# Sparse prompt attention taken head by head, with wide value products

## The chip, the cores and the metric

The kernel runs on one core of a Trainium2 chip. The metric is the device time of one execution in microseconds (us), as the median of several runs; lower is better. The core has a matmul engine (TensorE, PE in the rows, with its weight loads as PEld), a vector engine (VectorE, DVE), an activation engine (ScalarE, ACT), GpSimd (POOL) and a sync engine (SyncE, SP), which in this kernel issues almost all loads. Each engine works through its own list of instructions in order; they meet only through semaphores.

## The reference

One inference step of a four-layer decoder: gated linear attention (layer 0), sparse softmax attention (layer 1), a pooling mixer (layer 2) and gated linear attention again (layer 3). It is computed for a prompt of 512 tokens and for 8 x 4 sample tokens that look back on 1024 cached positions in pages. The change lies in layer 1, in the attention of the prompt:

```
def sparse_attend(q, k_sel, v_sel, valid):
    s = jnp.einsum('bqhd,bqkhd->bqhk', q, k_sel) * (DSA_HEAD_DIM ** -0.5)
    s = jnp.where(valid[:, :, None, :], s, -jnp.inf)
    p = jax.nn.softmax(s, axis=-1)
    return jnp.einsum('bqhk,bqkhd->bqhd', p.astype(v_sel.dtype), v_sel)

def dsa_out(o, g, w_out):
    B, L = o.shape[:2]
    return (o.reshape(B, L, DSA_WIDTH) * jax.nn.silu(g)) @ w_out
```

There are 8 heads of 128 numbers; each query keeps the 128 keys that an indexer scores highest among those not after it. The kernel does not gather keys for the prompt: it scores all keys that are not after the query's tile and adds a bias of -1e30 to those that were not chosen.

## The kernel before

**Units.** The 512 queries are four tiles of 128 (t = 0 to 3). A unit is one query tile of one head: 32 units. A unit of tile t has t + 1 key tiles. The list `UNITS` (lines 80 and 81) sets the order for every engine: four heads at a time of one query tile, the eight groups being (1, heads 0 to 3), (3, 0 to 3), (0, 0 to 3), (2, 0 to 3), then (0, 4 to 7), (1, 4 to 7), (2, 4 to 7), (3, 4 to 7).

**Steps of a unit.** `scores(n)` (PE, L1405) multiplies queries and keys, a product of 128(t + 1) columns; `shift(n)` (DVE, L2628 and L2633) adds the bias, writes `att_p` and takes the row maximum; the exponential (ACT, L2006) follows; `normalise(n)` (DVE, L2639 and L2641) divides by the row sum; `probs(n)` (PE, L1413) turns the t + 1 blocks of 128 x 128; `pt_out(n)` (ACT, L1979, in the profile the helper's line L1532) copies the turned blocks from PSUM to `att_pt`; `values_of(n)` (PE, L1424) multiplies them with the values, t + 1 products of 128 columns. Each fp32 product shows as two matmul passes in the trace, each turn as one.

**Groups of four units.** Four units fill one PSUM bank of 512 columns. Then comes the branch: DVE multiplies with the gate (L2649), ACT writes the high part `h_hi` (`branch_hi`, L1985, shown as L1532), DVE the low part `h_lo` (L2239). DVE waits for ACT between its two instructions.

**Order in time.** All engines run one loop over n. In step n, PE does scores(n), then a value page if there is one, then probs(n-2), then values_of(n-3). DVE does shift(n), normalise(n-1), and in every fourth step a branch. ACT does the exponential of n, pt_out(n-2), and in every fourth step branch_hi.

**Value pages.** Between the units PE works for the sample tokens. In the steps n = 0, 1, 3, 5 ... 29 it multiplies one page of cached values for each of four sequences (`value_page`, L1441): 16 steps with a page, each taking four transfers of 512 KB that SP issues as buffers come free. After the 8th and 16th page come the products with the new keys (L1448); in step 15 the sample probabilities of the second group are turned (L1380, L1382), in steps 17 and 33 the sample output (`turn_out`, L1458).

**After it.** `out_proj` multiplies the gated output with the output weights: three products for each of 8 k-blocks of 128 (one k-block is one head), L780 to L782. Its first half of the tokens (columns 0 to 271) waits for the branch of group (2, heads 4 to 7), its second for the last branch. In step 31 ACT also splits the first output weights (`w_hi`, L1532, 128x1024), from which POOL computes `w_lo` (L744).

Of the kernel before, what the change touches and what calls it, by code (L numbers as in the profile page):

```python
# [14 lines left out]
F32 = mybir.dt.float32  # L15
# [3 lines left out]
ALU = mybir.AluOpType  # L19
# [59 lines left out]

QUADS = [(1, 0), (3, 0), (0, 0), (2, 0), (0, 1), (1, 1), (2, 1), (3, 1)]  # L80
UNITS = [(t, 4 * half + h) for t, half in QUADS for h in range(4)]

# [11 lines left out]
def program(nc, plan, x_prompt, x_sample, state_gla, cache_k, cache_v, cache_idx_k, state_pool, page_table,  # L94
# [5 lines left out]
    with ExitStack() as ctx:  # L100
# [150 lines left out]
        v_end = d.o  # L251
        bias_p = [None] + [d(f"dsa_bias{t}", [P, P * (t + 1)]) for t in range(1, NP_T)]
        bias_s = d("dsa_bias_s", [NS, KEYS], BF16)
        ast = d("dsa_ast", [P, 5, 4])
# [7 lines left out]
        kst_at = d.o  # L262
        k_st = d("dsa_k_st", [P, TILES, BLK])
        tmp_d = d("dsa_tmp", [P, BLK])
        tmp_d2 = d("dsa_tmp2", [P, 8 * NS])
# [15 lines left out]
        a = Region(kst_at, kst_end)  # L281
        p_at = a("att_p", [P, 3, BLK])
        pt_at = a("att_pt", [P, 2, BLK])
        a = Region(pt_s_at, kst_end)
# [469 lines left out]
        def _(pe):  # L754
# [171 lines left out]
            def out_proj(L, between=None):  # L926
                last = L == len(KINDS) - 1

                def ready(k, part):
                    if KINDS[L] == 2:  # L930
                        pe.wait_ge(*on("h_lo", L, "y", k))
                    elif KINDS[L] == 0 and part == 0 and k % 4 == 0:
                        pe.wait_ge(*on("h_lo", (L, "out"), 2, k // 4))
                    elif k == 0 and KINDS[L] == 0:
                        pe.wait_ge(*on("h_lo", (L, "out"), SMP, 1))
                    elif k == 0:
                        pe.wait_ge(*on("h_lo", (L, "out"), *(QUADS[-2] if part == 0 else (SMP, 1))))

# [278 lines left out]
            def dsa(L):  # L1217
# [190 lines left out]
                def probs(n):  # L1408
                    t, h = units[n]
                    b = claim(2 + n % 2, ("PT", L, n), ("PT_read", L, n))  # L1410
                    pe.wait_ge(*on("p_norm", L, n))
                    for s in range(t + 1):
                        mm = pe.transpose(psum[:, b, s * P:(s + 1) * P], p_at[:, n % 3, s * P:(s + 1) * P], ident[:])  # L1413
                    mm.then_inc(*sig("PT", L, n))

                def values_of(n):
                    t, h = units[n]
                    m = n // 4
                    b = 4 + m % 2
                    if n % 4 == 0:  # L1420
                        claim(b, ("O", L, m), ("oT_read", L, t, h // 4))
# [40 lines left out]
                for n in range(N + 3):  # L1462
                    if n == 2 * NPAGE - 1:
                        turn_probs(1, (0, 1, 2))
                    if n in (2 * NPAGE + 1, 4 * NPAGE + 1):
                        turn_out(n // (4 * NPAGE))
                    if n < N:
                        scores(n)
                    if (n == 0 or n % 2) and n < 4 * NPAGE - 1:
                        value_page((n + 1) // (2 * NPAGE), (n + 1) // 2 % NPAGE)  # L1470
                    if 2 <= n <= N + 1:
                        probs(n - 2)
                    if n >= 3:
                        values_of(n - 3)
                out_proj(L)
# [54 lines left out]
        def _(act):  # L1530
# [277 lines left out]
            def dsa(L):  # L1808
# [165 lines left out]
                def pt_out(n):  # L1974
                    t, h = units[n]
                    act.wait_ge(*on("PT", L, n))
                    if n >= 2:
                        act.wait_ge(*on("O", L, n - 2))
                    copy(pt_at[:, n % 2, 0:(t + 1) * P], psum[:, bank_of("PT", L, n), 0:(t + 1) * P])\  # L1979
                        .then_inc(*sig("PT_read", L, n))  # L1980

                def branch_hi(m):
                    t, h = units[4 * m]
                    act.wait_ge(*on("oT_read", L, t, h // 4))
                    copy(H[L % 2][0][:, h:h + 4, cols(t)], tmp_d[:].rearrange("p (k t) -> p k t", k=4))\  # L1985
                        .then_inc(*sig("h_hi", (L, "out"), t, h // 4))

# [3 lines left out]
                for n in range(len(units) + 4):  # L1991
# [10 lines left out]
                    if n < len(units):  # L2002
                        t, h = units[n]
                        act.wait_ge(*on("s_shift", L, n))
                        x = p_at[:, n % 3, 0:(t + 1) * P]
                        act.activation(x, x, ACT.Exp, bias=ast[:, n % 3, 1:2], scale=score_scale[:, 0, t:t + 1],  # L2006
# [85 lines left out]
        def _(dve):  # L2092
# [124 lines left out]
            def resid(L):  # L2217
# [15 lines left out]
                input_lo(L + 1, *order[-1])  # L2233

            def out_lo(L, t, half, tmp):
                k = slice(4 * half, 4 * half + 4)
                dve.wait_ge(*on("h_hi", (L, "out"), t, half))
                hi, lo = H[L % 2]
                dve.tensor_tensor(lo[:, k, cols(t)], tmp.rearrange("p (k t) -> p k t", k=4),  # L2239
                                  hi[:, k, cols(t)].bitcast(F32), ALU.subtract)\  # L2240
                    .then_inc(*sig("h_lo", (L, "out"), t, half))


# [241 lines left out]
            def dsa(L):  # L2485
# [135 lines left out]
                def shift(n):  # L2621
# [4 lines left out]
                    if n >= 3:  # L2626
                        dve.wait_ge(*on("PT", L, n - 3))
                    dve.tensor_tensor_reduce(out=p_at[:, n % 3, 0:w], in0=psum[:, bank_of("S", L, n), 0:w],  # L2628
                                             in1=(bias_p[t][:] if t else future_p[:]), scale=1.0, scalar=TAKEN,
# [6 lines left out]
                def normalise(n):  # L2636
                    t, h = units[n]
                    dve.wait_ge(*on("p_exp", L, n))
                    link(dve.reciprocal(ast[:, n % 3, 3:4], ast[:, n % 3, 2:3]))  # L2639
                    x = p_at[:, n % 3, 0:(t + 1) * P]  # L2640
                    dve.tensor_scalar(x, x, ast[:, n % 3, 3:4], None, ALU.mult).then_inc(*sig("p_norm", L, n))  # L2641

                def branch(m):
                    t, h = units[4 * m]
                    dve.wait_ge(*on("O", L, 4 * m + 3))
                    if m:
                        pt, ph = units[4 * m - 4]
                        dve.wait_ge(*on("h_lo", (L, "out"), pt, ph // 4))
                    dve.tensor_tensor(tmp_d[:].rearrange("p (k t) -> p k t", k=4),  # L2649
                                      psum[:, 4 + m % 2, :].rearrange("p (k t) -> p k t", k=4),  # L2650
                                      gate_d[:, h:h + 4, cols(t)], ALU.mult).then_inc(*sig("oT_read", L, t, h // 4))
                    out_lo(L, t, h // 4, tmp_d[:])

# [136 lines left out]
```

## Time and profile before

| | us |
|---|---|
| median of 3 runs | 1143.22 |
| lowest and highest | 1142.87 and 1147.44 |
| profiled execution | 1143.32 |
| its span in the trace | 1141.6 |
| PE busy in it | 1107.5 (97%) |
| DVE busy | 669.8 (59%) |
| ACT busy | 490.9 (43%) |
| POOL busy | 381.8 (33%) |

The busy time of an engine is the time in which any of its instructions runs. Matmuls overlap, so the busy share of PE says little about how full it is; the distance from one start to the next is what a matmul costs. The stretch that the change touches lies from 576.4 us (first scores) to about 670 us of the span. In it the transfers of the cached values run as well.

### The profile page before, as it was taken

What the parts mean: (1) busy time and instruction counts of PE and PEld (TensorE: products, weight loads), DVE (VectorE), ACT (ScalarE), POOL (GpSimd) and SP (SyncE); (2) the same over time, 40 slices, a digit from 0 to 9 for tenths busy, and PEclk for the clock granted to TensorE, in tenths of its full rate; (3) what the DMA queues carried; (4) which work ended last, traced back from release to release, by engine and by line L of the source; (5) the groups of instructions that cost most, each with busy time, mean ns of one, the idle gap of its engine ahead of it and who ended that gap; (6) DMA issues with size and microseconds to landing.
All of it is one profiled execution on the core that took longest, in us unless ns stands there. A gap on an engine that the chain in (4) does not pass through costs nothing. (4 is left out here: it accounts for less than half of the span.)

```text
span 1141.6 us, 25758 instructions
## 1 busy us (share of the span) xinstructions
PE 1107.5 (97%) x10659; PEld 967.4 (85%) x10659; DVE 669.8 (59%) x1215; ACT 490.9 (43%) x960; POOL 381.8 (33%) x321
## 2 busy tenths in 40 slices
PE   8999999899999999999998999999999999999997
PEld 6889888899758988878954599999999889988796
DVE  6362355854999789677444646596455272255742
ACT  6542376643434222222364554332454352467643
POOL 5545122243313423114300044354335245312330
PEclk9999999999999999999999999999999999999998
DMA  5235234232315776894779942233220335233302
GB/s 177 99 112 166 92 111 147 97 100 87 118 46 185 240 266 212 272 319 147 259 292 409 373 125 79 71 111 95 101 94 3 111 112 157 84 130 112 105 26 79
DMA packets 126747, 168.97 MB, mean 148 GB/s; under 512 B 19336, under 2 KB 92336, under 8 KB 126623
## 3 DMA queue, kind: packets, MB, share of 16 engines
q1 hardware_dynamic: 114569, 152.75, 40.1%
q10 hardware_dynamic: 12062, 14.59, 3.6%
q8 instruction: 84, 1.38, 0.5%
q14 instruction: 32, 0.26, 0.1%
HBM read 150.86 MB, written 16.81 MB: 147 GB/s over the span
## 5 line engine op out<-in xcount | busy, mean ns | idle before, releaser
L744 POOL TENSOR_TENSOR w_lo<-raw,w_hi 128x512 fp32r<-128x512 f32 x265 | 358.0, 1383 | 681.0 <-ACT w_hi L1532 680.8
L780 PE MATMUL psum<-h_hi,w_hi 128*128 128x272 f32 x1584 | 462.0, 292 | 6.3 <-DVE h_lo L2449 4.7
L782 PE MATMUL psum<-h_hi,w_lo 128*128 128x272 f32 x1584 | 458.0, 289 | 0.0
L781 PE MATMUL psum<-h_lo,w_hi 128*128 128x272 f32 x1584 | 455.7, 288 | 0.0
L780 PEld LDWEIGHTS psum<-h_hi,w_hi 128*128 128x128 f32 x1584 | 297.3, 188 | 19.8 <-issue 14.7
L781 PEld LDWEIGHTS psum<-h_lo,w_hi 128*128 128x128 f32 x1584 | 297.7, 188 | 0.1
L782 PEld LDWEIGHTS psum<-h_hi,w_lo 128*128 128x128 f32 x1584 | 296.9, 187 | 0.0
L1532 ACT ACTIVATE w_hi<-raw 128x1024 fp32r<-128x1024 f32 (+1 forms) x135 | 133.3, 1033 | 111.5 <-PE psum L782 77.1
L780 PE MATMUL psum<-w_hi,h_hi 128*128 128x512 f32 (+2 forms) x352 | 124.6, 354 | 0.0
L782 PE MATMUL psum<-w_hi,h_lo 128*128 128x512 f32 (+2 forms) x352 | 121.0, 344 | 0.7 <-issue 0.7
L781 PE MATMUL psum<-w_lo,h_hi 128*128 128x512 f32 (+2 forms) x352 | 121.1, 344 | 0.4 <-issue 0.4
L2560 DVE STREAM_TRANSPOSE smp_keys<-smp_keys 128x2048 f32<-128x2048 f32 x32 | 73.1, 2301 | 34.1 <-DMA smp_keys<-in_cache_k_dram 33.8
L2227 DVE TENSOR_TENSOR XT<-psum,XT 128x272 f32<-128x272 f32 x64 | 27.9, 440 | 87.9 <-PE psum L782 87.9
L780 PEld LDWEIGHTS psum<-w_hi,h_hi 128*128 128x128 f32 (+1 forms) x352 | 64.0, 182 | 15.5 <-issue 5.8
L782 PEld LDWEIGHTS psum<-w_hi,h_lo 128*128 128x128 f32 (+1 forms) x352 | 64.1, 182 | 9.4 <-issue 0.5
L781 PEld LDWEIGHTS psum<-w_lo,h_hi 128*128 128x128 f32 (+1 forms) x352 | 64.1, 182 | 7.8
L1532 ACT ACTIVATE h_hi<-XT,gains 128x272 fp32r<-128x272 f32 x48 | 25.1, 523 | 75.1 <-DVE XT L2227 75.1
L1345 PE MATMUL psum<-smp_keys,raw 32*32 32x256 f32 x2048 | 46.2, 385 | 4.6 <-DVE smp_keys L2560 2.4
L1345 PEld LDWEIGHTS psum<-smp_keys,raw 32*32 32x32 f32 x2048 | 29.4, 103 | 16.4 <-issue 7.0
L2158 DVE TENSOR_TENSOR sq_sum<-sq_sum,sq_new 128x272 f32<-128x272 f32 x54 | 42.3, 783 | 1.5 <-ACT sq_new L1605 1.5
L1532 ACT ACTIVATE gla_s_now<-gla_s_now,gla_fac 128x256 f32<-128x256 f32 x64 | 27.2, 496 | 34.7 <-DVE gla_s_now L2332 25.9
L2549 DVE MAX8 dsa_top<-dsa_score_s 32x8 f32<-32x1056 f32 x32 | 39.6, 1238 | 0.8
(333 smaller groups left out, 1381.5 us busy)
## 6 DMA issues: line engine op xcount, KB each, us to landing
smp_keys<-in_cache_k_dram SPq DMA_DIRECT2D x128, 256.0 KB, 4.5
raw<-in_gla_w_in_dram SPq DMA_DIRECT2D x23, 1024.0 KB, 5.4
raw<-in_dsa_w_in_dram SPq DMA_DIRECT2D x17, 1024.0 KB, 5.5
spare<-in_cache_v_dram SPq DMA_DIRECT2D x34, 512.0 KB, 8.1
raw<-in_cache_v_dram SPq DMA_DIRECT2D x30, 512.0 KB, 8.4
gla_s_in<-in_state_gla_dram SPq DMA_DIRECT2D x16, 512.0 KB, 7.7
raw<-in_gla_w_out_dram SPq DMA_DIRECT2D x8, 1024.0 KB, 6.6
out_dram<-gla_s_in ACTq DMA_DIRECT2D x16, 512.0 KB, 4.7
```

The source lines that it names most:

```text
L744: pool.tensor_tensor(pair_view(w_lo, key)[:, k], raw_view(key)[:, k], pair_view(w_hi, key)[:, k].bitcast(F32), ALU.subtract)\
L780: pe.matmul(out, lh, rh, start=start, stop=False)
L781: pe.matmul(out, lh, rl, start=False, stop=False)
L782: return pe.matmul(out, ll, rh, start=False, stop=stop)
L1345: mm = pe.matmul(psum[band(c), 2 + i, 0:2 * P], q_bands[band(i), j, c, bl, :], keys[band(i), :, c, j, :], start=first and j == 0, stop=Fal ...
L1532: return act.activation(out, in_, ACT.Copy, scale=scale)
L2158: dve.tensor_tensor(sq_sum[:, c], sq_sum[:, c], sq_new[:, blocks(L).index((m, part)) % 2, :], ALU.add)\
L2227: dve.tensor_tensor(XT[:, m, c], psum[:, bank_of("proj", name, part), 0:HC], XT[:, m, c], ALU.add)\
L2549: link(dve.max(out=top8[0:m, :], in_=scores))
L2560: dve.transpose(held(s), held(s)).then_inc(*sig("kt_s", L, u))
```

## The change

The units are taken head by head, each head with tiles 1, 2, 3, 0. The four units of a head are copied into one buffer `att_pt` of 5 x 384 columns, so laid out that the turned probabilities of all query tiles that see key tile x stand side by side: 512 columns for x = 0, then 384, 256 and 128. `values_of` is called once a head, in the steps n = 6, 10 ... 34, with four products of these widths in place of ten of 128 columns. The first copy of a head waits until the value products of the head before are done. The branch works on one head and all 512 tokens, and `out_proj` waits for the branch of each head at its k-block, in the first half of the tokens. The third `att_p` buffer now lies where `bias_s` was. The numbers of passes and columns of scores and turns are the same as before.

```diff
-QUADS = [(1, 0), (3, 0), (0, 0), (2, 0), (0, 1), (1, 1), (2, 1), (3, 1)]
-UNITS = [(t, 4 * half + h) for t, half in QUADS for h in range(4)]
+UNITS = [(t, h) for h in range(DH) for t in (1, 2, 3, 0)]
...
-        pt_at = a("att_pt", [P, 2, BLK])
+        p_at = [a("att_p0", [P, BLK]), a("att_p1", [P, BLK]), at("att_p2", [P, BLK], F32, bias_s_at)]
+
+        pt_at = a("att_pt", [P, 5, BLK - P])
+        pt_row = pt_at[:].rearrange("p a b -> p (a b)")
...
+                    elif KINDS[L] == 1 and part == 0:
+                        pe.wait_ge(*on("h_lo", (L, "out"), "head", k))
                     elif k == 0:
-                        pe.wait_ge(*on("h_lo", (L, "out"), *(QUADS[-2] if part == 0 else (SMP, 1))))
+                        pe.wait_ge(*on("h_lo", (L, "out"), SMP, 1))
...
-                    pe.wait_ge(*on("PT_read", L, n))
-                    for s in range(t + 1):
-                        mm = pe.matmul(psum[:, b, (h % 4) * P:(h % 4 + 1) * P], v_d[:, s, h * HD:(h + 1) * HD],
-                                       pt_at[:, n % 2, s * P:(s + 1) * P], start=s == 0, stop=s == t)
-                    mm.then_inc(*sig("O", L, n))
+                def values_of(h):
+                    b = claim(4 + h % 2, ("O", L, h), ("oT_read", L, h))
+                    pe.wait_ge(*on("PT_read", L, NP_T * h + NP_T - 1))
+                    for x in range(NP_T):
+                        mm = pe.matmul(psum[:, b, x * P:], v_d[:, x, h * HD:(h + 1) * HD],
+                                       pt_row[:, x * BLK:x * BLK + BLK - x * P], start=x == 0, stop=x == NP_T - 1,
+                                       skip_group_check=True)
+                    mm.then_inc(*sig("O", L, h))
...
-                    if n >= 3:
-                        values_of(n - 3)
+                    if n >= 6 and n % NP_T == 2:
+                        values_of((n - 6) // NP_T)
...
-                    if n >= 2:
-                        act.wait_ge(*on("O", L, n - 2))
+                    if n and n % NP_T == 0:
+                        act.wait_ge(*on("O", L, n // NP_T - 1))
+                    c = t * P % (BLK - P)
+                    copy(pt_at[:, t // 3:t // 3 + t + 1, c:c + P],
...
+                def branch(h):
+                    dve.wait_ge(*on("O", L, h))
+                    if h:
+                        dve.wait_ge(*on("h_lo", (L, "out"), "head", h - 1))
+                    dve.tensor_tensor(tmp_d[:], psum[:, 4 + h % 2, :], gate_d[:, h, 0:SEQ], ALU.mult)\
+                        .then_inc(*sig("oT_read", L, h))
```

**PE between two value pages.** The names: `dsa_k,dsa_q` are scores, `ident,att_p` turns, `att_pt,dsa_v` values, `spare,smp_pt` or `raw,smp_pt` a value page. Before, steps 25 to 27:

```order
L1405 MATMUL psum<-dsa_k,dsa_q 128x384
L1441 MATMUL psum<-spare,smp_pt 32x512 x8
L1413 MATMUL psum<-ident,att_p 128x128 x2
L1424 MATMUL psum<-att_pt,dsa_v 128x128 x2
L1405 MATMUL psum<-dsa_k,dsa_q 128x384
L1413 MATMUL psum<-ident,att_p 128x128 x3
L1424 MATMUL psum<-att_pt,dsa_v 128x128 x2
L1405 MATMUL psum<-dsa_k,dsa_q 128x384
L1441 MATMUL psum<-raw,smp_pt 32x512 x8
```

The same steps now:

```order
L1410 MATMUL psum<-dsa_k,dsa_q 128x384
L1443 MATMUL psum<-spare,smp_pt 32x512 x8
L1418 MATMUL psum<-ident,att_p_162 128x128
L1410 MATMUL psum<-dsa_k,dsa_q 128x512
L1418 MATMUL psum<-ident,att_p_160 128x128 x2
L1425 MATMUL psum<-att_pt,dsa_v 128x512
L1425 MATMUL psum<-att_pt,dsa_v 128x384
L1425 MATMUL psum<-att_pt,dsa_v 128x256
L1425 MATMUL psum<-att_pt,dsa_v 128x128
L1410 MATMUL psum<-dsa_k,dsa_q 128x128
L1443 MATMUL psum<-raw,smp_pt 32x512 x8
```

Every second gap between two pages now holds the value products of a whole head, the others none.

**PE behind the last value page.** Before, from the products with the new keys (`dsa_v,smp_ptn`) to the last value product, which `out_proj` follows; `ident,smp_p` is `turn_out`:

```order
L1448 MATMUL psum<-dsa_v,smp_ptn 32x512 x8
L1413 MATMUL psum<-ident,att_p 128x128 x3
L1424 MATMUL psum<-att_pt,dsa_v 128x128 x3
L1405 MATMUL psum<-dsa_k,dsa_q 128x512
L1413 MATMUL psum<-ident,att_p 128x128 x4
L1424 MATMUL psum<-att_pt,dsa_v 128x128 x3
L1405 MATMUL psum<-dsa_k,dsa_q 128x512
L1413 MATMUL psum<-ident,att_p 128x128 x4
L1424 MATMUL psum<-att_pt,dsa_v 128x128 x4
...
L1458 MATMUL psum<-ident,smp_p_151 128x128 x8
L1413 MATMUL psum<-ident,att_p 128x128 x4
L1424 MATMUL psum<-att_pt,dsa_v 128x128 x8
```

And now:

```order
L1450 MATMUL psum<-dsa_v,smp_ptn 32x512 x8
L1418 MATMUL psum<-ident,att_p_160 128x128
L1410 MATMUL psum<-dsa_k,dsa_q 128x512
L1418 MATMUL psum<-ident,att_p_161 128x128 x2
L1425 MATMUL psum<-att_pt,dsa_v 128x512
...
L1410 MATMUL psum<-dsa_k,dsa_q 128x128
L1418 MATMUL psum<-ident,att_p_162 128x128 x3
L1418 MATMUL psum<-ident,att_p_160 128x128 x4
L1460 MATMUL psum<-ident,smp_p_151 128x128 x8
L1418 MATMUL psum<-ident,att_p_161 128x128
L1425 MATMUL psum<-att_pt,dsa_v 128x512
...
```

Behind the last page stand now 5 score tiles, 11 turns and the values of two heads (20 tiles), before 8, 19 (with one row of four left out above) and 22.

**ACT at the end.** `h_hi<-dsa_tmp` is branch_hi, `w_hi<-raw` the split of the output weights. Before:

```order
L2006 ACTIVATE att_p,dsa_ast<-att_p,dsa_ast,score_scale 128x512
L1532 ACTIVATE att_pt<-psum 128x512
L1532 ACTIVATE h_hi<-dsa_tmp 128x4x128
L1532 ACTIVATE w_hi<-raw 128x1024 x2
L1532 ACTIVATE att_pt<-psum 128x512 x2
```

Now:

```order
L2008 ACTIVATE att_p_161,dsa_ast<-att_p_161,dsa_ast,score_scale 128x128
L1534 ACTIVATE att_pt<-psum 128x3x128
L1534 ACTIVATE h_hi<-dsa_tmp 128x512
L1534 ACTIVATE w_hi<-raw 128x1024 x2
L1534 ACTIVATE att_pt<-psum 128x4x128
L1534 ACTIVATE att_pt<-psum 128x128
```

The places are the same; the last unit is now a small one, and all value products of the last head come behind its copy.

## Rows read from the trace of the kernel before

**Rows 1.** The page's head: span.

```profile
span 1141.6 us, 25758 instructions
```

**Rows 2.** Busy time by stretch; us, engines, granted clock, DMA share, GB/s.

```profile
core 0: us, PE busy (x) PEld busy (x) DVE busy (x) ACT busy (x) POOL busy (x), PEclk, DMA share, GB/s
...
590.00:610.00 20.00, 17.93 (x137) 10.77 (x130) 10.31 (x40) 8.77 (x22) 0.00 (x0) 1.00 1.03 409
...
620.00:640.00 20.00, 19.26 (x154) 10.95 (x147) 12.18 (x57) 9.75 (x30) 0.00 (x0) 1.00 1.02 402
```

**Rows 3.** Waits from 588 to 615 us: total, times, longest.

```profile
PE psum L1441 <- DMA raw<-in_cache_v_dram: 1.9, 2, 1.1
...
PE psum L1441 <- DMA spare<-in_cache_v_dram: 1.0, 2, 0.7
```

**Rows 4.** PE in order of time: start, us, instruction, [idle before <-releaser].

```profile
610.01 1.92 PE L1441 MATMUL psum<-raw,smp_pt 128*32 128x512 f32 x16 [1.09 <-DMA raw<-in_cache_v_dram]
...
625.85 1.92 PE L1441 MATMUL psum<-spare,smp_pt 128*32 128x512 f32 x16
...
649.53 1.02 PE L1405 MATMUL psum<-dsa_k,dsa_q 128*128 128x512 f32 x2
650.40 0.49 PE L1413 MATMUL psum<-ident,att_p 128*128 128x128 f32 x3
650.72 0.83 PE L1424 MATMUL psum<-att_pt,dsa_v 128*128 128x128 f32 x6
651.39 1.02 PE L1405 MATMUL psum<-dsa_k,dsa_q 128*128 128x512 f32 x2
652.35 0.62 PE L1441 MATMUL psum<-raw,smp_pt 128*32 128x512 f32 x2
...
656.05 0.55 PE L1413 MATMUL psum<-ident,att_p 128*128 128x128 f32 x3
...
657.11 1.02 PE L1405 MATMUL psum<-dsa_k,dsa_q 128*128 128x512 f32 x2
...
665.54 2.05 PE L1424 MATMUL psum<-att_pt,dsa_v 128*128 128x128 f32 x16 [0.34 <-ACT att_pt L1532]
667.34 0.37 PE L780 MATMUL psum<-h_hi,w_hi 128*128 128x272 f32 x1
```

**Rows 5.** Line L1413 (turns) in two stretches: PE, PEld busy (x), clock, DMA.

```profile
625.85:652.35 26.50, 4.91 (x24) 2.92 (x24) 1.00 0.98 379
652.35:667.34 14.99, 3.01 (x19) 2.12 (x19) 1.00 0.50 159
```

**Rows 6.** Line L1424 (value passes) in the same two stretches.

```profile
625.85:652.35 26.50, 7.32 (x48) 6.42 (x48) 1.00 0.98 379
652.35:667.34 14.99, 5.76 (x44) 5.24 (x44) 1.00 0.50 159
```

**Rows 7.** Waits from 576 to 676 us, DVE for ACT in the branch.

```profile
DVE h_lo L2239 <- ACT h_hi L1532: 10.2, 8, 1.7
```

**Rows 8.** DVE in order of time, at the end.

```profile
658.17 0.69 DVE L2628 CUSTOM_DVE_ANT_0 att_p<-psum,dsa_bias 128x512 f32<-128x512 f32 x1 [4.17 <-PE psum L1405]
...
661.08 0.15 DVE L2639 RECIPROCAL dsa_ast<-dsa_ast 128x1 f32<-128x1 f32 x1
...
661.67 0.68 DVE L2649 TENSOR_TENSOR dsa_tmp<-psum,dsa_gate 128x512 f32<-128x512 f32 x1
...
669.02 0.81 DVE L2239 TENSOR_TENSOR h_lo<-dsa_tmp,h_hi 128x512 fp32r<-128x512 f32 x1 [0.70 <-ACT h_hi L1532]
```

**Rows 9.** ACT in order of time, at the end.

```profile
662.49 0.62 ACT L1532 ACTIVATE h_hi<-dsa_tmp 128x512 fp32r<-128x512 f32 x1
663.01 1.99 ACT L1532 ACTIVATE w_hi<-raw 128x1024 fp32r<-128x1024 f32 x2
664.90 1.07 ACT L1532 ACTIVATE att_pt<-psum 128x512 f32<-128x512 f32 x2
```

**Rows 10.** Weight loads of the value passes, 576 to 676 us: busy, mean ns.

```profile
L1424 PEld LDWEIGHTS psum<-att_pt,dsa_v 128*128 128x128 f32 x160 | 20.5, 193 | 1.5 <-ACT att_pt L1532 0.9 <-issue 0.5
```

More of the change, by code:

```diff
@@ L252, in program @@
         bias_p = [None] + [d(f"dsa_bias{t}", [P, P * (t + 1)]) for t in range(1, NP_T)]
+        bias_s_at = d.o
         bias_s = d("dsa_bias_s", [NS, KEYS], BF16)
@@ L263, in program @@
         k_st = d("dsa_k_st", [P, TILES, BLK])
+        d.o += size([P, P], F32)
         tmp_d = d("dsa_tmp", [P, BLK])
@@ L281, in program @@
         a = Region(kst_at, kst_end)
-        p_at = a("att_p", [P, 3, BLK])
-        pt_at = a("att_pt", [P, 2, BLK])
+        p_at = [a("att_p0", [P, BLK]), a("att_p1", [P, BLK]), at("att_p2", [P, BLK], F32, bias_s_at)]
+        pt_at = a("att_pt", [P, 5, BLK - P])
+        pt_row = pt_at[:].rearrange("p a b -> p (a b)")
         a = Region(pt_s_at, kst_end)
@@ L1412, in probs @@
                     for s in range(t + 1):
-                        mm = pe.transpose(psum[:, b, s * P:(s + 1) * P], p_at[:, n % 3, s * P:(s + 1) * P], ident[:])
+                        mm = pe.transpose(psum[:, b, s * P:(s + 1) * P], p_at[n % 3][:, s * P:(s + 1) * P], ident[:])
                     mm.then_inc(*sig("PT", L, n))
[L1416 to L1421, printed above, removed]
-                    pe.wait_ge(*on("PT_read", L, n))
-                    for s in range(t + 1):
-                        mm = pe.matmul(psum[:, b, (h % 4) * P:(h % 4 + 1) * P], v_d[:, s, h * HD:(h + 1) * HD],
-                                       pt_at[:, n % 2, s * P:(s + 1) * P], start=s == 0, stop=s == t)
-                    mm.then_inc(*sig("O", L, n))
+                def values_of(h):
[6 more added lines that the diff above has]
+                    mm.then_inc(*sig("O", L, h))
                 def value_page(grp, pg):
@@ L1976, in pt_out, with branch_hi @@
                     act.wait_ge(*on("PT", L, n))
-                    if n >= 2:
-                        act.wait_ge(*on("O", L, n - 2))
-                    copy(pt_at[:, n % 2, 0:(t + 1) * P], psum[:, bank_of("PT", L, n), 0:(t + 1) * P])\
-                        .then_inc(*sig("PT_read", L, n))
[L1982 to L1986, printed above, removed]
+                    if n and n % NP_T == 0:
+                        act.wait_ge(*on("O", L, n // NP_T - 1))
+                    c = t * P % (BLK - P)
+                    copy(pt_at[:, t // 3:t // 3 + t + 1, c:c + P],
+                         psum[:, bank_of("PT", L, n), 0:(t + 1) * P].rearrange("p (x q) -> p x q", q=P))\
+                        .then_inc(*sig("PT_read", L, n))
+                def branch_hi(h):
+                    act.wait_ge(*on("oT_read", L, h))
+                    copy(H[L % 2][0][:, h, 0:SEQ], tmp_d[:]).then_inc(*sig("h_hi", (L, "out"), "head", h))
                 for q in (KT - 2, KT - 1):
@@ L2004, in dsa @@
                         act.wait_ge(*on("s_shift", L, n))
-                        x = p_at[:, n % 3, 0:(t + 1) * P]
+                        x = p_at[n % 3][:, 0:(t + 1) * P]
                         act.activation(x, x, ACT.Exp, bias=ast[:, n % 3, 1:2], scale=score_scale[:, 0, t:t + 1],
@@ L2233, in resid @@
                 input_lo(L + 1, *order[-1])
[L2235 to L2241, printed above, removed]
             def gla(L):
@@ L2627, in shift @@
                         dve.wait_ge(*on("PT", L, n - 3))
-                    dve.tensor_tensor_reduce(out=p_at[:, n % 3, 0:w], in0=psum[:, bank_of("S", L, n), 0:w],
+                    dve.tensor_tensor_reduce(out=p_at[n % 3][:, 0:w], in0=psum[:, bank_of("S", L, n), 0:w],
                                              in1=(bias_p[t][:] if t else future_p[:]), scale=1.0, scalar=TAKEN,
@@ L2639, in normalise @@
                     link(dve.reciprocal(ast[:, n % 3, 3:4], ast[:, n % 3, 2:3]))
-                    x = p_at[:, n % 3, 0:(t + 1) * P]
+                    x = p_at[n % 3][:, 0:(t + 1) * P]
                     dve.tensor_scalar(x, x, ast[:, n % 3, 3:4], None, ALU.mult).then_inc(*sig("p_norm", L, n))
[L2643 to L2652, printed above, removed]
+                def branch(h):
[4 more added lines that the diff above has]
+                        .then_inc(*sig("oT_read", L, h))
+                    hi, lo = H[L % 2]
+                    dve.wait_ge(*on("h_hi", (L, "out"), "head", h))
+                    dve.tensor_tensor(lo[:, h, 0:SEQ], tmp_d[:], hi[:, h, 0:SEQ].bitcast(F32), ALU.subtract)\
+                        .then_inc(*sig("h_lo", (L, "out"), "head", h))
                 for n in range(len(units) + 4):
```

## The prediction

> **What bounds the kernel now.** First the page's head and the times: the profiled execution took 1143.32 us, of which the span is 1141.6 [rows 1]; the 1.7 us around it stay. The median of the runs shown, 1143.22, is 0.1 us below this execution, so the sum is made against 1143.3.
>
> Second, the busy time by stretch [rows 2]. Between 590 and 640 us the transfers are busy all the time (share 1.02 to 1.03, 402 to 409 GB/s). One value page is 4 x 512 KB = 2.1 MB, at 408 GB/s 5.1 us. Third: who waits for whom between 588 and 615 us [rows 3]. PE waits for value pages four times, 2.9 us in all, and the last wait ends at 610.01, at the 8th page [rows 4]. Up to there the transfers set the pace. After it no value page begins with a wait for a transfer: PE has become the slower one, and it stays so.
>
> Fourth, PE in order of time [rows 4], read by distances of starts, since busy times overlap. Scores of 512 columns are two passes in 650.40 - 649.53 = 0.87 us, or 0.435 a pass and 0.109 for 128 columns. Three turns take 650.72 - 650.40 = 0.32, 0.107 each. Six value passes of 128 columns take 651.39 - 650.72 = 0.67, 0.112 each. A value page takes 1.85 (half of the 3.70 from 652.35 to 656.05, in which a page and the equally long products with the new keys stand). DVE and ACT have idle time there, but their latency shows at the end: at 665.54 PE waits for the last copy, then the last value passes run and out_proj starts at 667.34. From 667.34 on PE is busy without a gap for long, so a later out_proj is a later end of the kernel, one for one.
>
> **The change part by part.** The kernel is cut at 610.01, 625.85 (10th page), 652.35 (16th page) and 667.34.
>
> *Fewer, wider value passes.* 160 passes of 128 columns (80 tiles by two) become 64. One head costs 2 x (512+384+256+128)/512 x 0.435 = 2.18 us; ten tiles narrow cost 20 x 0.112 = 2.24. That is 0.06 a head, 0.4 us for all eight. The weight loads that go (96 of 193 ns, [rows 10]) ran beside passes that start every 112 ns, so they save nothing more.
>
> *Up to 610.01.* A head now costs PE between two equal points two pages 3.7, ten score tiles 2.18, ten turns 1.07, the values 2.18 and about 0.3 of changes between kinds of work: 9.4 us, against 10.3 us for the transfers of two pages. So the 8th page still waits for its transfer, with some 0.8 us to spare. 0 us; bounds -0.3 (the wait was 1.1 and cannot turn into a gain, the next transfer has its own time) and +1.0 (if the first head, whose exponentials start late, stalls).
>
> *610.01 to 625.85.* Scores of steps 14 to 17: before tiles 3, 3, 1, 1 = 8, now 4, 1, 2, 3 = 10: +0.44. Turns 10 and 10. Values: before units 10 to 13 = 8 tiles, 16 x 0.112 = 1.79, now head 2 = 2.18: +0.39. In step 17 turn_out must wait until DVE has read the scores of step 16, and DVE does this behind a branch, in which it stands 10.2 / 8 = 1.3 us for ACT [rows 7]. Before, value passes of 0.67 us stood in PE's list ahead of turn_out; now none do. I take +0.6 (bounds 0 and 1.2). Sum +1.4.
>
> *625.85 to 652.35.* This is the cleanest comparison. The page steps are 17 and 29. Scores are 30 tiles before and after. Turns: 24 before [rows 5], now those of units 15 to 26 in the new order, 30: +0.64. Values: 48 passes before [rows 6], 5.38 us, now heads 3, 4, 5 = 6.54: +1.16. So PE reaches the last page with more of the units done, 1.8 us later. A loop beside it: turn, copy, branch_hi, the low part, the next two maxima, the exponential, the copy, the values. By the durations of the kinds of rows shown in [rows 8, 9] it comes to about 9.5 us a head, as long as PE's own 9.4. I add 0.2. Sum +2.0 (bounds 0 and 4).
>
> *652.35 to 667.34: 14.99 us before.* What was done earlier is now missing here: 5 score tiles in place of 8, 11 turns in place of 19, 20 value tiles in place of 22. By PE's work alone, 3.70 + 5 x 2 x 0.109 + 11 x 0.107 + 2 x 2.18 + turn_out's eight turns 0.95 = 11.3 us, 3.7 us less. But the chain cannot be that short. From the page's start: 3.70; turn 0.17, scores of unit 30 0.87, two turns 0.22, head 6 2.18, scores of unit 31 0.22: 7.4. DVE, 0.2 later, needs about 0.5 for the small maximum and its scaling, 0.59 for normalising unit 30 (661.08 to 661.67, [rows 8]) and 0.68 for the branch of head 6: 9.4. ACT: branch_hi 0.52 (662.49 to 663.01), the split of the weights 1.89 (663.01 to 664.90), the copies of units 30 and 31 some 0.5 and 0.25 [rows 9]: 12.7. Then all four products of head 7, 2.18: 14.9. So out_proj begins 14.9 after the page, -0.1 us. All the work taken out of this stretch becomes waiting. Bounds -1.5 (if ACT comes by its branch_hi earlier) and +2 (if the copy of unit 31 meets a late DVE).
>
> *out_proj's new waits.* The k-block of head 7 is the last of eight; it is asked for 21 products later, 2.6 us at the measured rate of three products per 0.375. Before, from 667.34 to the end of the last low part (669.02 + 0.81 = 669.83, [rows 8]) 2.5 us pass. It just fits: 0, bounds 0 and +0.5. Gate, branch and low part have the same number of elements, and the copy to `att_pt` the same columns: 0.
>
> Sum: 0 + 1.4 + 2.0 - 0.1 = +3.3, on the span 1144.9, as a time 1146.6. Against the median shown this is +3.4, or 0.3%.
>
> A rule of the Trainium skill speaks against this sum. Its page "TensorE: Matmul & The Clock Gate", section "Back-to-back issue gap", says that in a stream of weight loads and matmuls the spacing comes from both, about 81 ns for 128 columns and about 131 ns for 512; a wide one would be only 1.6 times as dear as a narrow one. The rows show 435 against 112 ns, 3.9 times, so the trace does not agree for this fp32 work; by the rule a head's values would fall from 2.24 to an estimated 1.2 us.
>
> **The rivals.**
> *Transfers still set the pace after 610 us, or the slack of the waits swallows the work moved.* Then the last page stays at about 652.4 and only the tail counts. For it: the DMA share of 1.02 up to 640, and the steps of the pages are more even now. Against it: no wait of PE for a transfer after 610.01, and PE's list between the pages grew. Result 1143.3 - 0.1 = 1143.2, within a tie.
> *Wide passes are much cheaper.* If a pass had a fixed part so large that a wide one costs half as much per column, head values drop by 1.1 us; six heads lie behind 610.01, -6.6 in all, of which the end, bound by latency, gives back one head only. About 1146.6 - 5.5 = 1141. For it only that 112 is above 109; against it the 435 of the scores. This is the case that the rule above would give. It goes over to faster by 0.5% only if the tail shrinks too.
> *The loop of DVE and ACT becomes the bound: slower.* ACT waits in the first copy of each head for the value products of the head before, and behind this wait stand the exponential of the small unit, the next copy and branch_hi; DVE stands in the branch until that comes; PE's turns and values wait for both. The place is the copy of each head's first unit. It decides from the point where the loop is longer than PE's 9.4 us a head plus what a page may wait. If every latency is a tenth longer, a head takes 10.4: four and a half heads behind 610.01 give +4.5, to 1151. For it: the loop's own 9.5. Against: the wait of ACT ends before the next maximum is there, by my sum by 0.4 us.
>
> **How the numbers follow.** A measurement of this kernel can tell 0.5%, that is 5.7 us (below 1137.5 or above 1148.9), from no change. Forecast 0.64, at 1146.6 with its own range 1144.5 to 1148.9; transfers as the bound 0.18; cheap wide passes 0.05; the loop 0.13. Faster: of the cheap passes a part and some ill-sized tail, 0.04. Slower: most of the loop and the upper end of the forecast, 0.13. Same: the rest, 0.83. The range takes in the tie and part of the loop: 1142.3 to 1150.2.
>
> **What would show it.** In the new trace the 8th page should start within 1 us of 610 behind a wait for a transfer; the 10th at 627.3; the 16th at 655.7; out_proj 14.9 behind it, at 670.6. Value passes: 64, a wide one 0.43 apart. In the tail PE should show about 3 us of idle time that ends with ACT's copies or DVE's normalisation, and before the k-block of head 7 none or a few tenths. Wrong would be: a 16th page before 653.5 (the transfers or slack had it), or value passes of 512 columns nearer than 0.3 us, or a head from page to page longer than 10 us (the loop), or an out_proj more than 2 us off 14.9 behind the last page.

## The result and the profile after

| | before | changed |
|---|---|---|
| median of 20 runs each | 1143.30 | 1148.93 |
| lowest and highest | 1141.59 and 1147.44 | 1146.14 and 1151.90 |
| profiled execution | 1143.32 | 1146.14 |
| its span | 1141.6 | 1144.4 |

The ratio is 1.0044, with a 95% interval of 1.0036 to 1.0052: slower by 4.1 to 5.9 us. That is less than the 0.5% taken as the bound, but it is not nothing. The profiled execution is the shortest of the twenty. It stands 2.8 us above the one profiled before, where 3.3 were forecast; the median stands 5.6 above. The median also stands at the upper edge of the forecast's own 1144.5 to 1148.9. So two things have to be explained: whether the 2.8 is made of the parts that were forecast, and where the rest comes from.

The head of the page, which answers to [rows 1]:

```profile
span 1144.4 us, 25546 instructions
```

Busy time by stretch of the changed kernel, as in [rows 2]:

```profile
590.00:610.00 20.00, 17.62 (x111) 8.83 (x112) 10.46 (x40) 8.59 (x22) 0.00 (x0) 1.00 1.03 409
620.00:640.00 20.00, 18.10 (x116) 8.48 (x109) 11.59 (x50) 8.82 (x23) 0.00 (x0) 1.00 0.97 362
```

Up to 610 us the transfers run at 409 GB/s as before; between 620 and 640 they move 362 in place of 402. PE asks for pages later there, so they are not the bound. Its waits for transfers, from 588 to 615 us, answer to [rows 3]:

```profile
PE psum L1443 <- DMA raw<-in_cache_v_dram: 2.2, 2, 1.5
...
PE psum L1443 <- DMA spare<-in_cache_v_dram: 1.7, 1, 1.7
```

PE in order of time, from the 8th page (609.48) to `out_proj` (670.06), answers to [rows 4]:

```profile
609.48 1.92 PE L1443 MATMUL psum<-raw,smp_pt 128*32 128x512 f32 x16 [0.71 <-DMA raw<-in_cache_v_dram]
...
624.31 1.06 PE L1460 MATMUL psum<-ident,smp_p 128*128 128x128 f32 x8 [1.39 <-DVE dsa_ast L2621]
625.88 0.91 PE L1410 MATMUL psum<-dsa_k,dsa_q 128*128 128x384 f32 x2 [0.51 <-DVE dsa_tmp L2576]
626.72 1.92 PE L1443 MATMUL psum<-spare,smp_pt 128*32 128x512 f32 x16
...
629.82 2.32 PE L1425 MATMUL psum<-att_pt,dsa_v 128*128 128x512 f32 x8
631.98 0.39 PE L1410 MATMUL psum<-dsa_k,dsa_q 128*128 128x128 f32 x2
...
655.29 0.62 PE L1443 MATMUL psum<-raw,smp_pt 128*32 128x512 f32 x2
...
662.62 0.49 PE L1418 MATMUL psum<-ident,att_p 128*128 128x128 f32 x3
664.11 0.63 PE L1418 MATMUL psum<-ident,att_p 128*128 128x128 f32 x4 [1.00 <-DVE att_p L2634]
664.57 1.04 PE L1460 MATMUL psum<-ident,smp_p 128*128 128x128 f32 x8
666.50 0.30 PE L1418 MATMUL psum<-ident,att_p 128*128 128x128 f32 x1 [0.89 <-DVE att_p L2634]
667.91 2.40 PE L1425 MATMUL psum<-att_pt,dsa_v 128*128 128x512 f32 x8 [1.12 <-ACT att_pt L1534]
670.06 0.37 PE L783 MATMUL psum<-h_hi,w_hi 128*128 128x272 f32 x1
```

The 10th page starts 17.24 us behind the 8th, the 16th 28.57 behind the 10th, `out_proj` 14.77 behind the 16th. Before, these were 15.84, 26.50 and 14.99. In the tail PE now stands 1.00 + 0.89 + 1.12 = 3.01 us, of which DVE's normalisation ends two parts and ACT's last copy one. Between 626.72 and 655.29 no row of PE shows an idle time.

Lines L1418 (turns) and L1425 (value passes) in the last two stretches, as in [rows 5, 6]; the first two rows are the turns:

```profile
626.72:655.29 28.57, 5.57 (x30) 3.68 (x30) 1.00 0.82 307
655.29:670.06 14.77, 2.13 (x11) 1.34 (x11) 1.00 0.62 204
...
626.72:655.29 28.57, 7.11 (x24) 4.32 (x24) 1.00 0.82 307
655.29:670.06 14.77, 4.47 (x16) 2.83 (x16) 1.00 0.62 204
```

24 passes are those of heads 3, 4 and 5, 16 those of heads 6 and 7. The groups of value passes by shape, and DVE's wait in the branch, which answers to [rows 7]:

```profile
L1425 PE MATMUL psum<-att_pt,dsa_v 128*128 128x512 f32 x16 | 8.4, 607 | 1.1 <-ACT att_pt L1534 1.1
L1425 PE MATMUL psum<-att_pt,dsa_v 128*128 128x384 f32 x16 | 6.5, 486 | 0.0
```

```profile
DVE h_lo L2644 <- ACT h_hi L1534: 11.2, 8, 1.6
```

From here on "the stage" is what lies between its first scores and the first product of `out_proj`. All times in the table are distances of starts on PE, in us. A dip is a stretch in which the granted clock falls to 0.50, half of full speed (1.2 GHz in place of 2.4).

| profile | to 8th page | 8th to 10th | 10th to 16th | 16th to out_proj | stage |
|---|---|---|---|---|---|
| before | 33.65 | 15.84 | 26.50 | 14.99 | 90.98 |
| before, again | 33.39 | 15.84 | 26.49 | 15.00 | 90.72 |
| changed | 33.94 | 17.24 | 28.57 | 14.77 | 94.52 |
| changed, second | 32.63 | 17.24 | 28.56 | 14.78 | 93.21 |
| changed, third (dip) | 33.46 | 17.24 | 28.56 | 16.45 | 95.71 |
| changed, fourth (dip) | 34.15 | 17.24 | 28.56 | 15.81 | 95.76 |

### The profile page after: what moved, and what is told of

Same layout as the page of the kernel before. It is cut to its first block and busy times, and to the rows that moved or that the text cites. A ratio compares the mean times of both kernels' runs of the same rounds, so it can differ in the third digit from the quotient of the medians.

```text
span 1144.4 us, 25546 instructions
## 1 busy us (share of the span) xinstructions
PE 1105.9 (97%) x10563; PEld 961.1 (84%) x10563; DVE 669.3 (58%) x1215; ACT 491.9 (43%) x960; POOL 381.5 (33%) x321
## 5 line engine op out<-in xcount | busy, mean ns | idle before, releaser
L783 PEld LDWEIGHTS psum<-h_hi,w_hi 128*128 128x128 f32 x1584 | 297.3, 188 | 19.9 <-issue 14.7
```

What stands on the lines that cost most here:

```text
L783: pe.matmul(out, lh, rh, start=start, stop=False)
```

## The experiments

**The same kernels again** (after_again, after_third, after_fourth; before_again), with no edit.

> The changed kernel once more. Theory A (the forecast's steps hold; what the median shows above them is a lower TensorE clock for a few us in part of the executions): the stretch from the first scores to out_proj takes 94.5 us again (90.98 before), and executions above 1148 show a mean clock of 0.994 to 0.995, those near 1146.5 one of 0.996 or more. Theory B (the loop of DVE and ACT, or the transfers, run slower in part of the executions): an execution above 1148 shows this stretch 2 to 4 us longer at a granted clock of 1.00.

> The kernel before once more. Theory A: 1143.3 us, and a mean clock of 0.996 to 0.998 in nearly all executions. Theory B says nothing of the clock and expects the stretch at 91 us in each.

On one chip, beside 20 runs of before with a median of 1142.86: changed 1147.14 (1.0038, 1.0026 to 1.0049), before once more 1143.92 (1.0011, 0.9998 to 1.0024). So a difference of 0.1% between two sets is nothing, and the 0.38% is something. The distances between the pages repeat to 0.01 us; only the part up to the 8th page, where transfers are waited for, scatters.

Of the two theories put on record for the slow executions, the sign of the first, a lower clock, came in the twenty executions of the result: nine have a mean clock of 0.995 or less, all of them above 1148, and the seven below 1148 are at 0.996 or more. It did not come in after_again: four of its ten executions stand above 1148, all at 0.997. So the clock is not all that separates them. B, that the stage is 2 to 4 us longer at a clock of 1.00, was seen in no profile.

> The changed kernel as it is, on the same chip as the other three: the stretch from the first scores to out_proj 93 to 94.5 us, the pieces behind the 8th page 17.2, 28.6 and 14.8 us again. Time 3 to 5 us above the kernel before.

On a second chip 1148.85 (1.0046, 1.0031 to 1.0060). Its profile was the surprise. PE's last value products, and the stretches around them (us, busy time of PE, PEld, DVE, ACT, POOL, granted clock, DMA share, GB/s):

```profile
667.23 0.30 PE L1418 MATMUL psum<-ident,att_p 128*128 128x128 f32 x1 [0.89 <-DVE att_p L2634]
668.64 4.07 PE L1425 MATMUL psum<-att_pt,dsa_v 128*128 128x512 f32 x8 [1.11 <-ACT att_pt L1534]
672.47 0.37 PE L783 MATMUL psum<-h_hi,w_hi 128*128 128x272 f32 x1
```

```profile
664.00:665.00 1.00, 0.16 (x2) 0.19 (x3) 0.96 (x4) 1.00 (x4) 0.00 (x0) 1.00 0.61 202
...
666.00:667.00 1.00, 0.34 (x4) 0.10 (x1) 0.96 (x3) 1.00 (x2) 0.02 (x1) 1.00 0.05 17
667.00:668.00 1.00, 0.30 (x1) 0.14 (x1) 0.74 (x9) 1.00 (x2) 1.00 (x1) 1.00 0.00 0
668.00:669.00 1.00, 0.35 (x1) 0.39 (x2) 0.00 (x0) 0.80 (x3) 1.00 (x2) 0.81 0.00 0
669.00:670.00 1.00, 1.00 (x2) 0.45 (x2) 0.00 (x0) 0.00 (x0) 1.00 (x2) 0.50 0.00 0
```

PE idled 1.00, 0.89 and 1.11 us between short pieces of work, as in the first profile; then the clock fell to 0.50, up to 672. The eight passes took 672.47 - 668.64 = 3.83 us where the first profile has 2.15: +1.68.

The same thing happens ahead of the stage, where nothing was changed. Both orders have a wait of PE there of 2.15 to 2.2 us, ahead of 128 products of the sample tokens. In the first profile the clock is 0.50 behind it, from 510.6 to 514.0; in the one of before it stays at 1.00:

```profile
510.33 4.05 PE L1350 MATMUL psum<-smp_keys,raw 32*32 32x256 f32 x128 [2.15 <-DVE smp_keys L2553]
```

```profile
511.93 2.75 PE L1345 MATMUL psum<-smp_keys,raw 32*32 32x256 f32 x128 [2.17 <-DVE smp_keys L2560]
```

These 128 products take 1.30 us longer. Of the fourteen profiles in this document six have a dip behind this wait: after, after_again, after_third, half_after, both and half_before, which has another at 497.

> The changed kernel as it is, beside the one with the added turns, on the same chip: 3 to 5.5 us above the kernel before, a third of the executions with a mean clock of 0.995 or less.

On a third chip 1148.60 (1.0049, 1.0033 to 1.0066). It dips in the same place, at 672.3 in its time; the clock is back during 675 to 676. 1.04 us of the price stand before `out_proj` and about 0.65 in its first products (the span behind the start of `out_proj` is 475.00, against 474.34 in the first profile): 1.7 in all. Two of its six executions have a mean clock of 0.995 or less, the third that was expected.

**narrow: the same order, but ten narrow products a head.**

```diff
-for x in range(NP_T):  # 512, 384, 256, 128 columns
-    mm = pe.matmul(psum[:, b, x * P:], v_d[:, x, ...], pt_row[:, x * BLK:x * BLK + BLK - x * P], ...)
+for t in range(NP_T):
+    for x in range(t + 1):
+        c = x * BLK + (t - x) * P
+        mm = pe.matmul(psum[:, b, t * P:(t + 1) * P], v_d[:, x, ...], pt_row[:, c:c + P], ...)
```

> The changed kernel with ten value products of 128 columns a head in place of four of 512 to 128 (all else as changed). Forecast's term: +0.06 us a head, so +0.4 us in all against the changed kernel, of which the part before 610 us hides behind transfers: about 1149.2, no difference to be told. The rival of cheap wide passes: +5 us or more, about 1154.

```profile
631.62 2.40 PE L1427 MATMUL psum<-att_pt,dsa_v 128*128 128x128 f32 x20
633.85 0.39 PE L1410 MATMUL psum<-dsa_k,dsa_q 128*128 128x128 f32 x2
```

A head of 20 narrow passes takes 633.85 - 631.62 = 2.23 us, one of eight wide passes 631.98 - 629.82 = 2.16. Width is worth 0.07 a head. From the 8th page to `out_proj` narrow takes 61.02, the changed kernel 60.58. By these profiles the new order carries the whole loss, and the wide products give back a few tenths of a microsecond. The median of narrow is 1149.66 (1.0054, 1.0036 to 1.0072; five executions), 2.5 above after_again's on the same chip. The products' width doesn't account for that much; its profile begins the stage at 577.82, after_again's at 575.33, ahead of all that differs between them.

**early_split: the weights split one step earlier**, so that the last two copies don't stand behind it in ACT's list.

```diff
+if n == len(units) - 2:      # ACT, ahead of the exponential
+    split_hi(pair_of[(L, "out", 0)])
...
-if n == len(units) - 1:
-    split_hi(pair_of[(L, "out", 0)])
```

> The changed kernel with ACT's split of the first output weights moved from step 31 to ahead of the exponential of step 30. If ACT's order ends the tail, as the forecast says, the copies of units 30 and 31 no longer stand behind 1.9 us of split: out_proj starts about 14.0 us behind the last value page in place of 14.8, time -0.9 us. If DVE's normalising and branch end it alone: no change, or +0.3 us since the exponential of unit 30 comes later.

It missed. The tail became longer, 15.72 in place of 14.77, at a clock of 1.00 (median 1149.84). The copy of unit 30 did come sooner, but DVE was now late, and PE waited 1.68 and 1.81 us for it. Rows of DVE and POOL in order of time:

```profile
663.07 0.89 DVE L2634 TENSOR_SCALAR att_p<-att_p,dsa_ast 128x512 f32<-128x512 f32 x1
...
665.25 1.61 DVE L2644 TENSOR_TENSOR h_lo<-dsa_tmp,h_hi 128x512 fp32r<-128x512 f32 x1 [0.70 <-ACT h_hi L1534]
...
661.17 5.14 POOL L747 TENSOR_TENSOR w_lo<-raw,w_hi 128x512 fp32r<-128x512 f32 x4 [83.92 <-ACT w_hi L1534]
```

The same two DVE instructions take 0.49 and 0.69 us in the changed kernel, where POOL starts only at 666.3. Beside POOL's `w_lo` they take 0.40 and 0.92 more. The branch on PSUM, `dsa_tmp`, kept its 0.68. This fits a sentence of the Trainium skill ("SBUF — State Buffer", "SBUF: two separate sides"): VectorE and GpSimd share one pair of SBUF ports, which VectorE needs for some forms only (its fast two-port modes, or two inputs in SBUF beside a GpSimd instruction that reads SBUF), and the one that comes second is held up for the whole instruction of the other. No run kept the DVE instructions and took POOL's away, so the cause stays an argument from these rows. Besides, ACT waited 1.09 us for the raw weights, which had not landed.

**turn19: turn_out of the first group in step 19, not 17.**

```diff
-if n in (2 * NPAGE + 1, 4 * NPAGE + 1):     # PE and DVE
+if n in (2 * NPAGE + 3, 4 * NPAGE + 1):
```

> The changed kernel with the first turn_out (and DVE's work on it) two steps later, in step 19, behind the value products of head 3 in PE's list. The forecast's term: PE stood 1.39 us ahead of turn_out in step 17 for DVE's maximum of unit 16; this wait goes, the 0.5 us ahead of the next scores stays. From the 8th page to the 16th 44.4 us in place of 45.8, and the time -1.4 us. Rival (DVE and ACT's loop is the bound and the wait only moves): no change, 45.8.

```profile
628.68 1.04 PE L1460 MATMUL psum<-ident,smp_p 128*128 128x128 f32 x8
```

It now stands behind a head's value products and has no idle time ahead. From the 8th page to the 16th 44.37 us against 45.81: the 1.39 us wait has gone and comes back nowhere. Median 1146.07 (1.0022, 1.0008 to 1.0036), against 1148.85 for the changed kernel on the same chip. That is 2.8 less, where the stage shows 1.44; where the rest comes from is not shown.

**last_narrow: the last head's values unit by unit**; **both: this and turn19.**

```diff
-if n >= 6 and n % NP_T == 2:
+if 6 <= n < N + 2 and n % NP_T == 2:
     values_of((n - 6) // NP_T)
+if n >= N - 1:
+    last_values(n - 3)    # t + 1 products of 128 columns behind the unit's own copy
```

> The changed kernel with the values of head 7 alone in narrow products, unit by unit in steps 31 to 34, so that only the one tile of unit 31 and the four of unit 30 stand behind the last copies. If the tail is latency with PE idle, as forecast: from the 16th page to out_proj 13.7 in place of 14.8 us, time -1.1 us. If the low parts of the output weights (POOL, ready 5 us behind its start) hold out_proj instead: the gain is seen at its start and lost in its first products, 0.

> Both edits together: -2.5 us against the changed kernel, still about 1 us above the kernel before, since PE's order ahead of the last page stays as the change made it (28.6 against 26.5 us from the 10th to the 16th page).

```profile
666.08 0.30 PE L1418 MATMUL psum<-ident,att_p 128*128 128x128 f32 x1 [0.22 <-DVE att_p L2649]
667.23 1.38 PE L1438 MATMUL psum<-att_pt,dsa_v 128*128 128x128 f32 x10 [0.86 <-ACT att_pt L1549]
668.37 0.37 PE L783 MATMUL psum<-h_hi,w_hi 128*128 128x272 f32 x1
```

Above, last_narrow: half of the last head's passes now fill the two waits for DVE, and the tail takes 13.50 us. Its median, 1148.51, nevertheless stands only 0.3 below the changed kernel's, where 1.1 was expected. The profile shows why: the 1.27 us gained ahead of `out_proj` are lost again behind it, where the span is 475.73 in place of 474.34. The 51st product of `out_proj` starts 6.83 behind the first in place of 6.36: one weight load waits 0.22 us for POOL's `w_lo`, the rival that was expected, and the low part of the last head, beside POOL's work, takes 1.33 in place of 0.69 us. And 400 us later, in layer 3, PE waits longer for a transfer. The last two rows are this wait in the first profile of the changed kernel and in last_narrow:

```profile
670.04 1.33 DVE L2659 TENSOR_TENSOR h_lo<-dsa_tmp,h_hi 128x512 fp32r<-128x512 f32 x1 [0.70 <-ACT h_hi L1549]
```

```profile
1069.80 0.71 PE L1173 MATMUL psum<-gla_v_s,gla_k_seq 32*128 32x256 f32 x8 [0.33 <-DMA gla_s_in<-in_state_gla_dram]
```

```profile
1069.49 0.71 PE L1173 MATMUL psum<-gla_v_s,gla_k_seq 32*128 32x256 f32 x8 [1.30 <-DMA gla_s_in<-in_state_gla_dram]
```

The wait is 1.30, 1.42 and 1.28 us in last_narrow, both and fill, and at most 0.44 in the other eleven profiles; why these three have it is not shown. both has a stage of 91.20, 0.2 to 0.5 longer than before's, 475.81 behind it against 474.21, and a median of 1145.38 (1.0021, 1.0007 to 1.0036). No version beat the kernel before.

**fill: 24 idle turns in the tail's waits**, to ask whether they bring the dip.

```diff
+def fill(k):
+    for x in range(k):
+        pe.transpose(psum[:, 6, 0:P], ident[:], ident[:])
...
+if n == N: fill(8)
+if n == N + 1: fill(7)
+if n == N + 2: fill(9)      # ahead of the values
```

> The changed kernel with 24 more turns of the identity (8, 7 and 9), whose results nobody reads, put into PE's three waits of 1.0, 0.9 and 1.1 us behind the last value page. Theory A (in part of the executions PE's idle time there brings the clock down to half, and the last head's values take 3.8 us in place of 2.2): PE never idles there, so few executions show a mean clock below 0.996, and the median comes 1 to 2 us closer to the kernel before; a profile at full clock shows the tail at 14.8 to 15.1 us as without them. Theory B (the clock is not what separates the executions): median as of the changed kernel, or up to 0.5 us above it.

Median 1148.07, against 1148.60 for the changed kernel on the same chip: no difference that can be told, where the theory of the clock had 1 to 2 us. Its other sign came, with few executions: none of the five has a mean clock of 0.995 or less, against two of six. But fill also has the longer wait in layer 3, 0.9 us more, so its median decides little. In its profile the tail takes 14.78 at a clock of 1.00, but a dip came elsewhere, behind the waits at the first turn_out:

```profile
625.59 1.07 PE L1465 MATMUL psum<-ident,smp_p 128*128 128x128 f32 x8 [1.39 <-DVE dsa_ast L2632]
627.16 1.30 PE L1410 MATMUL psum<-dsa_k,dsa_q 128*128 128x384 f32 x2 [0.51 <-DVE dsa_tmp L2587]
628.39 3.18 PE L1443 MATMUL psum<-spare,smp_pt 128*32 128x512 f32 x16
```

```profile
624.00:626.00 2.00, 0.61 (x6) 0.44 (x5) 1.52 (x6) 0.65 (x2) 0.00 (x0) 1.00 1.02 401
...
627.00:628.00 1.00, 0.84 (x2) 0.30 (x2) 0.11 (x2) 0.00 (x0) 0.00 (x0) 0.78 1.01 401
628.00:630.00 2.00, 2.00 (x9) 0.40 (x12) 1.20 (x5) 0.65 (x2) 0.00 (x0) 0.50 1.03 412
```

It made the two distances 17.63 and 29.81, 0.39 and 1.25 longer: again 1.64. Nine profiles have these waits at the first turn_out, and this is the only one with a dip behind them. So there are two places with new waits, and a dip was seen behind each.

**half_before and half_after: half of the sample's value traffic.** Only one of the two transfers of each value item is made, and its data are multiplied twice, so half of the value pages is missing from the sample's result. PE's work is unchanged.

```diff
-for x in range(kk):                        # SP's loads
+for x in range(kk if kind == "K" else 1):
...
-o = (bl % 2) * D + half * BLK              # value_page
+o = half * BLK
```

> The kernel before with half the bytes of cached values: of the two pages in a buffer only the first is loaded, and both sequences' products read it (same instructions on PE). Forecast's theory (transfers set the pace up to the 8th page, PE behind it): only PE's waits for transfers go, 2.9 us in all, and the stretch from the first scores to out_proj is 88 us in place of 91. Rival (transfers are the bound up to the last page): 8 us or more go.

> The changed kernel with half the bytes of cached values in the same way. Forecast's theory: its waits for transfers (3.4 to 3.9 us) go, 90 to 90.5 us in place of 93.2 to 94.5, still 2 to 2.5 us above the half-loaded kernel before; the pieces behind the 8th page stay 17.2, 28.6 and 14.8 us. Rival (transfers): the two come out equal.

PE waits for no transfer in either stage. In the order before, the three distances are 15.84, 26.50 and 14.99; in the changed order 17.24, 28.56 and 16.21, the last with a dip. With twice the room on the transfers, the distances behind the 8th page are the same to 0.01 us, but for the one with the dip. Up to the 8th page they shrink to 30.48 and 29.98. Single runs: 1142.33 and 1145.33.

## Why the prediction was right, and what it missed

*Up to the 8th page: 0.* Right. It starts at 609.48 behind a wait of 0.71 for a transfer. In the four profiles of the changed kernel this part has a mean of 33.55, in the two of before 33.52. With half the traffic the changed order would even be the faster here, by 0.5; the transfers hide that.

*8th to 10th page: +1.4.* Measured 17.24 - 15.84 = 1.40. The pieces: turn_out waits 1.39 where a wait of 0.23 stood before, 1.16 more, at the upper bound given and not the 0.6 taken; the waits in step 15 (0.20 and 0.47 before, 0.35 now) gave 0.32 back. Waits together +0.84, work +0.56, where the forecast had +0.6 and +0.83. That the sum agrees to 0.03 is therefore luck: both parts are off by a quarter us, in opposite directions. turn19 shows that the wait is real time.

*10th to 16th page: +2.0.* Measured 2.07. The cause was right: 30 turns in place of 24, and three heads' values. But the 0.2 for the loop of DVE and ACT stands there under a wrong name, since PE's rows show no idle time. What it covered is, by elimination, change between kinds of work on PE: a head takes 645.72 - 636.15 = 9.57 us from page to page in the first profile, and I had 9.4.

*16th page to out_proj: -0.1.* Measured -0.22 (14.77 against 14.90 forecast), with 3.0 us of waiting. The forecast's own terms, 9.4 + 0.52 + 1.89 + 0.5 + 0.25 + 2.18, come to 14.7, not 14.9: the step to "12.7" is 0.1 to 0.2 too high. The step that says "All the work taken out of this stretch becomes waiting" is the useful one. A correction to it: I let ACT be the last engine, and of the three waits DVE's normalisation ends two.

*out_proj's new waits and wide passes: 0.* Right. Between 670.06 and 676 no row of PE has an idle time. That it just fits is shown by last_narrow: with `out_proj` nearer to POOL's and DVE's low parts its first products take 0.47 longer, close to the upper bound of 0.5. And 0.07 us a head was measured where 0.06 was worked out. So the spacing that the Trainium skill gives ("TensorE: Matmul & The Clock Gate", "Back-to-back issue gap"), by which a wide pass would be only 1.6 times as dear as a narrow one, does not hold for this fp32 work.

*The rivals.* Transfers as the bound is refuted by the half-traffic pair. Cheap wide passes are refuted by narrow. The loop as the bound is refuted by the gapless stretch from 626.72 to 655.29: ACT does wait for value products in its first copy (4.1 us in all, in 7 times), but PE never waits behind that.

*What was missed.* The sum has no term for the clock. The waits that the forecast itself put in, 1.39 + 0.51 at turn_out and 1.0 + 0.9 + 1.1 in the tail, are followed by a dip in part of the executions. The price is 1.64 to 1.7 us where it can be followed to its end. In the tail a dip is in the third, the fourth and half_after; narrow, early_split and turn19 have like waits there without one: 3 of 8 profiles. In the six profiles where these waits are short or filled (three in the order before, last_narrow, both, fill) the tail has none. All executions taken together say more. A mean clock of 0.995 or less is found in 23 of 65 executions of the versions with the waits in the tail (the changed kernel, narrow, early_split, turn19), in 2 of 27 where they are short or filled (last_narrow, both, fill), and in 4 of the 76 of the order before that have their clock on record. That ties the lower clock to these waits, with one exception: after_again has none in ten. The Trainium skill describes the like on "TensorE: Matmul & The Clock Gate", "A second HAM failure mode: psum-queue depth-cycling": short idles between groups of matmuls let the clock go back and forth, and the throughput falls though the median matmul is as fast as ever.

But the clock is only a part. Of the 46 executions of the changed kernel the 16 at 0.995 or less have a median of 1149.4, the other 30 one of 1147.7, while those of the order before at 0.996 or more stand at 1143.0. That leaves 4.7 where the mean clock shows nothing, though a single dip (1.7 us lost in 1144, or 0.0015) can hide in a mean of 0.996.

The books, profile against profile (means of four changed and two before): outside the span +0.2, ahead of the stage +0.65, the stage +3.95, behind it +0.3. In the stage, pages account for 3.47, the tail without its dips for -0.22, the dips for 0.68 (and 0.16 more behind it). Ahead of the stage nothing was changed, and the dip at 510 us, in three of the four changed profiles and in neither of the two of before, makes 3/4 x 1.30 = 0.98 there by itself. Whether that is chance can't be told; half_before has it too. The start of the stage also scatters without any dip ahead of it, from 575.22 in early_split to 578.74 in the fourth.

The 3.3 of the forecast and 0.85 for the dips in the stage make 4.1, the lower end of the measured 4.1 to 5.9. Up to 1.8 us stay unexplained; the profiles of the changed kernel show no place for them in the stage. So the forecast was right in its steps, each to 0.15 us. The 2.8 us of the profiled execution are 3.54 in the stage (0.29 of it up to the 8th page), 0.08 behind it, and -0.82 ahead of it, since that stage begins at 575.54 and not 576.36; so that they come near the forecast's 3.3 is in part luck. That the median, at 1148.93, still lay in the range of 1142.3 to 1150.2 is luck in part too: that range reached so far up for the sake of the loop, which is refuted. The version both, 2.45 above the kernel before, is explained for the most part: its profile has 1.6 of it behind `out_proj` and 0.2 to 0.5 in the stage.

## What to carry to other kernels

Where a stretch ends in a chain through several engines, moving matmuls ahead of it moves time, it does not save any: the pages in front become later by the full price of the work, and the chain behind stays as long, with idle time in it. Price a new wait on TensorE twice, once as idle time and once as the risk that the clock falls for the work behind it. When a source is reordered, look at the instruction that used to stand between a producer and its user (here value products ahead of turn_out): that was the cover, and putting it back (turn19) gave its 1.4 us back in full, up to the last page. And follow a gain to the end of the kernel: last_narrow won 1.27 us in its stage and lost 1.39 behind it.

## What the runs showed of the hardware that was not expected

- Three idles of 0.9 to 1.1 us, parted by work as short as one turn, were followed by a granted clock of 0.50 in 3 of 7 profiles, and by none in the others with the same idles to 0.01 us (the first, second, narrow and turn19). Of the profiles with one idle of 2.15 to 2.2 us at 510 us, 6 of 14 had a clock of 0.50 behind it. The same program dips or doesn't.
- At half the clock the eight fp32 value passes of a head took 3.83 us against 2.15, 1.78 times as long and not twice, since the clock was back at 672.0 and the passes ended at 672.47.
- VectorE instructions that read and write SBUF alone took 0.89 for 0.49 us and 1.61 for 0.69 us beside GpSimd's `w_lo`; one that reads PSUM kept its 0.68.
- fp32 passes of 128 and 512 columns cost by columns: 20 of 128 take 2.23 us, eight with the same columns in all 2.16.
